# Expert stage: sums leave PSUM on ScalarE and are added into x on GpSimd, which also makes the token matrix; inner activations are turned two units later

## What is computed

```
aff = softmax(h @ w_router);  g, idx = top_k(aff.T, 2 * n_tok // 16)     # 64 latent, 16 prompt tokens
xe = xt[idx]
hid = silu(xe @ w1) * (xe @ w3)                                         # 1024 -> 1024, for each expert
ye = (hid @ w2) * g
out = zeros.at[idx].add(ye);  x = x + gate2 * out
```

## Time and profile before

| | us |
|---|---|
| median of three runs | 3389.22 (3378.01 to 3390.41) |
| profiled execution | 3387.95 |
| its span | 3386.2 |
| PE, PEld, DVE, ACT, POOL busy | 2982.3, 2085.9, 2172.3, 1564.4, 217.2 |
| one pair of experts, fourth of layer 0 | 79.1 |

### The profile page before, as it was taken

One profiled execution on the slowest core, in us unless ns is written; L12 is line 12 of the kernel. 1 busy time (PEld: TensorE's weight loads), 2 busy tenths in 40 slices (PEclk: granted clock), 3 DMA queues, 4 the chain that ended last, 5 costly groups with the idle time before them and its releaser, 6 DMA issues.

```text
span 3386.2 us, 42584 instructions
## 1 busy us (share of the span) xinstructions
PE 2982.3 (88%) x14726; PEld 2085.9 (62%) x14726; DVE 2172.3 (64%) x3151; ACT 1564.4 (46%) x2258; POOL 217.2 (6%) x272
## 2 busy tenths in 40 slices
PE   6979988988977999999878899889799599999995
PEld 3656755766645666666646576556575366666663
DVE  3364345566437999999834553455752699999994
ACT  3151333123125777777533413331410377777773
POOL 0050011011000000000002300110200000000000
PEclk9989999999988999999989899999999699999996
DMA  7203200321416999999811031023012299999991
GB/s 265 81 1 110 76 27 26 114 76 51 156 56 225 332 326 329 320 332 328 288 65 57 26 135 51 1 75 113 28 38 94 102 341 325 319 329 322 329 338 58
DMA packets 280112, 564.04 MB, mean 167 GB/s; under 512 B 14040, under 2 KB 19872, under 8 KB 279328
## 3 DMA queue, kind: packets, MB, share of 16 engines
q1 hardware_dynamic: 273056, 543.33, 45.4%
q10 hardware_dynamic: 4448, 9.87, 0.8%
q0 software_dynamic: 2464, 8.91, 0.7%
HBM read 546.44 MB, written 15.63 MB: 166 GB/s over the span
## 4 chain that ended last, share of the span: by engine, by line
PE 66%; DVE 16%; ACT 6%; issue 5%; DVEq 4%; ACTq 2%; DMA 1%; POOL 0%; POOLq 0%; SPq 0%
PE mm L1423 17%; PE mm L931 14%; PE mm L868 11%; DVE w_lo L1913 6%; PE mm L933 4%; PE mm L1166 2%; DVEq L2451 2%; PE mm L965 2%; ACT w_hi L1482 2%; DVE x L1921 2%; ACTq L1851 2%; PE oo L1188 1%; DVE scratch L2102 1%; PE tp L1175 1%; PE oo L905 1%
## 5 line engine op out<-in xcount | busy, mean ns | idle before, releaser
L1913 DVE TENSOR_TENSOR w_lo<-ring,w_hi 128x1024 fp32r<-128x1024 f32 x768 | 919.1, 1221 | 87.8 <-ACT w_hi L1482 57.7
L1482 ACT ACTIVATE w_hi<-ring 128x1024 fp32r<-128x1024 f32 x768 | 803.5, 1059 | 288.4 <-PE mm L1423 266.5
L1913 DVE TENSOR_TENSOR dw_lo<-ring,dw_hi 128x512 fp32r<-128x512 f32 (+1 forms) x168 | 114.9, 689 | 420.4 <-ACT dw_hi L1482 420.1
L1482 ACT ACTIVATE dw_hi<-ring 128x512 fp32r<-128x512 f32 (+1 forms) x168 | 104.4, 627 | 548.3 <-PE mm L933 543.5
L931 PE MATMUL mm<-h_hi,dw_lo 128*128 128x512 f32 (+1 forms) x672 | 328.9, 489 | 19.2 <-DVE dw_lo L1913 13.1
L933 PEld LDWEIGHTS mm<-h,ring 128*128 128x128 f32 (+1 forms) x1344 | 256.3, 191 | 61.3
L931 PE MATMUL mm<-h_hi,dw_hi 128*128 128x512 f32 (+1 forms) x672 | 269.4, 401 | 0.0
L931 PE MATMUL mm<-h_lo,dw_hi 128*128 128x512 f32 (+1 forms) x672 | 268.0, 399 | 0.0
L933 PE MATMUL mm<-h,ring 128*128 128x128 f32 (+1 forms) x1344 | 260.9, 276 | 0.0
L868 PE MATMUL mm<-scratch,ring 128*128 128x512 f32 (+3 forms) x896 | 257.9, 440 | 1.6 <-ACT scratch L1482 1.6
L1423 PE MATMUL mm<-w_lo,xa_hi 128*80 128x512 f32 x512 | 204.6, 400 | 15.5 <-DVE w_lo L1913 9.5
(11 more groups left out here) (256 smaller groups left out, 5011.9 us busy)
## 6 DMA issues: line engine op xcount, KB each, us to landing
ring<-in_w_ff SPq DMA_DIRECT2D x384, 1024.0 KB, 6.0
ring<-in_w_ada SPq DMA_DIRECT2D x48, 1024.0 KB, 7.3
ring<-in_w_gate SPq DMA_DIRECT2D x24, 1024.0 KB, 5.8
ring<-in_w_in SPq DMA_DIRECT2D x16, 1024.0 KB, 8.9
ring<-in_w_o SPq DMA_DIRECT2D x8, 1024.0 KB, 7.4
x_spill<-x SPq DMA_DIRECT2D x2, 2560.0 KB, 13.0
ring<-in_w_br_da SPq DMA_DIRECT2D x4, 1024.0 KB, 6.3
ring<-in_w_br_mla SPq DMA_DIRECT2D x4, 1024.0 KB, 6.2
```

The source lines that it names most:

```text
L1482: return act.activation(out, in_, ACT.Copy, scale=scale)
L1913: return dve.tensor_tensor(out, in0, in1, op)
```

## The change

1. `TURN_AT` goes from 10, 18, 26, 34 to 12, 20, 28, 36. `SLOTS_AT` moves with it from 20 to 22, `ROWS_AT` stays at 38.
2. `spread` leaves VectorE. ScalarE copies the sum out of PSUM with the gate as its scale, into one of two buffers (`tmp[2]` and `rstd`), and GpSimd adds the buffer into x. ScalarE's copy k stands ahead of w_hi of unit 12+k and waits until GpSimd has done addition k-2. GpSimd's additions of units 2n and 2n+1 stand behind its wait for chunk n. The last pair's sums are still added by VectorE, after a wait for GpSimd.
3. `hot_t` is made by GpSimd behind chunk 11, when all combines of the pair before are done. TensorE's first combine and VectorE's `slots` wait for it.
4. `hidden` on VectorE has no drain any more and signals `hid_ready` directly. `mm_empty` is raised by TensorE behind its wait for `hid_ready`.

```diff
-TURN_AT = [JOB_UNITS * (q + 1) + 2 for q in range(4)]
-SLOTS_AT, ROWS_AT = TURN_AT[1] + 2, TURN_AT[3] + 4
+TURN_AT = [JOB_UNITS * (q + 1) + 4 for q in range(4)]
+SLOTS_AT, ROWS_AT = TURN_AT[1] + 2, TURN_AT[3] + 2
+SPREADS = (PAIRS - 1) * KT
...
+        def spread_at(k):
+
+            return (tmp[2], rstd)[k % 2][:, 0:NLAT]
...
+            pool.sem_inc(spread_done, 2)
...
-                def pair(e, last_pair=False):
+                def spread(k, of):
+
+                    pool.wait_ge(spread_in, l * SPREADS + of * KT + (k + 1))
+                    pool.sem_inc(pool_waited, 1)
+                    pool.tensor_tensor(x[:, k, 0:NLAT], x[:, k, 0:NLAT], spread_at(k), ALU.add).then_inc(spread_done, 1)
+
+                def pair(e, before=None, last_pair=False):
                     for n in range(PAIR_CHUNKS):
 
                         pool.wait_ge(w_ready, pair_part(l, e, n * UNITS + UNITS - 1))
                         pool.sem_inc(chunks_free, 1)
+                        if before is not None:
+                            for m in (UNITS * n, UNITS * n + 1):
+                                if 0 <= m - SPLITS - COMBINE_AT < KT:
+                                    spread(m - SPLITS - COMBINE_AT, before)
+                        if n == after(TURN_AT[AF1]):
+                            if before is not None:
+                                wait_o_full(pool, l, OO["pairs"] + KT - 1, before)
+                            pool.sem_inc(pool_waited, 1)
+                            pool.tensor_scalar(hot_t[:, :], tokens, slot_tok, 1.0, ALU.is_equal, ALU.mult)\
+                                .then_inc(hot_t_ready, 1)
                         if n == after(SLOTS_AT) + 1 and not last_pair:
                             fetch(e + 1)
...
                     if k == 0:
                         pe.wait_ge(ye_done, l * PAIRS + of + 1)
+                        pe.wait_ge(hot_t_ready, l * PAIRS + of + 1)
...
                     pe.wait_ge(hid_ready, (l * PAIRS + e) * 4 + (q + 1))
+                    pe.sem_inc(mm_empty[job_turn(q) % 2], 1)
...
+                def spread(k, of):
+
+                    j = OO["pairs"] + k
+                    act.wait_ge(spread_done, l * SPREADS + of * KT + (k + 1))
+                    wait_o_full(act, l, j, of)
+                    copy(spread_at(k), oo[j % 2][:, :], mod[:, 40 + k, 0:1]).then_inc(o_empty[j % 2], 1)
+                    act.sem_inc(spread_in, 1)
+
+                def hi_of_chunk(n, e, before=None):
...
+                            if before is not None and 0 <= p - COMBINE_AT < KT:
+                                spread(p - COMBINE_AT, before)
...
-                        if before is not None and 0 <= m - SPLITS - COMBINE_AT < KT:
-                            spread(m - SPLITS - COMBINE_AT, before)
...
                     tt(hid[0:rows_, n * 512:(n + 1) * 512], mm[j % 2][0:rows_, 512:1024], tmp[n][0:rows_, 0:512],
-                       ALU.mult).then_inc(mm_empty[j % 2], 1)
-                    dve.drain()
-                    dve.sem_inc(hid_ready, 1)
+                       ALU.mult).then_inc(hid_ready, 1)
...
-                            ts(hot_t[:, :], tokens, slot_tok, ALU.is_equal)
                             lo_of_hidden(AF1, e)
                         if n == after(SLOTS_AT) and not last_pair:
+                            dve.wait_ge(hot_t_ready, l * PAIRS + e + 1)
                             slots(T_SLOTS, e, e + 1)
...
+                dve.wait_ge(spread_done, (l + 1) * SPREADS + 2)
                 for k in range(KT):
                     spread(k, PAIRS - 1)
```

More of the change, by code:

```diff
@@ L540, in build @@
         pool_waited = sem("pool_waited")
+        spread_in, spread_done = sem("spread_in"), sem("spread_done")
         xhi_ready, xe_ready = sem("xhi_ready"), sem("xe_ready")
@@ L544, in build @@
         ye_stored, ye_back, ye_done = sem("ye_stored"), sem("ye_back"), sem("ye_done")
-        ye_hi_ready = sem("ye_hi_ready")
+        ye_hi_ready, hot_t_ready = sem("ye_hi_ready"), sem("hot_t_ready")
         y_ready, y_sent = sem("y_ready"), sem("y_sent")
@@ L843, in _ @@
                 fetch(0)
-                with pool.Fori(0, PAIRS - 1) as e:
-                    pair(e)
-                pair(PAIRS - 1, True)
+                pair(0)
+                with pool.Fori(1, PAIRS - 1) as e:
+                    pair(e, e - 1)
+                pair(PAIRS - 1, PAIRS - 2, True)
         @block.tensor
@@ L1796, in _ @@
                 copy(hotw_pt.rearrange("p g s -> p (g s)"), tp[:, 0:2 * P]).then_inc(t_empty, 1)
-                def hi_of_chunk(n, e, last_pair=False):
+                def spread(k, of):
[5 more added lines that the diff above has]
+                def hi_of_chunk(n, e, before=None):
                     i = AT[l, "pairs"] + n
@@ L1855, in pair @@
                     for n in range(2, PAIR_CHUNKS if last_pair else PAIR_CHUNKS + 2):
-                        hi_of_chunk(n, e, last_pair)
+                        hi_of_chunk(n, e, before)
                         if n == 2 and before is not None:
@@ L2413, in outputs, with lo_of_chunk @@
                         dve.sem_inc(ye_done, 1)
-                def lo_of_chunk(n, e, before=None):
+                def lo_of_chunk(n, e):
                     i = AT[l, "pairs"] + n
@@ L2463, in pair @@
                     for n in range(2, PAIR_CHUNKS if last_pair else PAIR_CHUNKS + 2):
-                        lo_of_chunk(n, e, before)
+                        lo_of_chunk(n, e)
                         if n == 2 and before is not None:
```

## The result

The changed kernel takes 3449.14 us (median of 4 runs, 3446.87 to 3451.89), the one before 3389.1 beside it. The ratio is 1.0184, 95% interval 1.0164 to 1.0204: 1.8% slower, 60 us, where the forecast had 3437 us and a range up to 3475. The profiled run took 3446.87 us, its span 3445.1. Ratios in this document leave out one run of 11,389 us, among four of the version with the old turns, whose other three took 3494 to 3497.

What follows compares the result with a forecast made beforehand. TensorE was taken to set the pace, VectorE close behind. 14 pairs with sums at +3.9 us (+54.6) and two first pairs at -3 (-6) gave +49 on 3387.95, so 3437 us; range 3380 to 3475.

Steps and rivals of the forecast that it cites:

- The start of the loop: Expert stage, w_lo of unit 13 on VectorE: claimed to end near 1301.3 us, no longer behind an addition.
- The loop: Units 12 to 19: w_lo, GpSimd addition, ScalarE copy, w_hi in a chain, 5.8 us per two units against TensorE's 3.7.
- wake: GpSimd's delay between the end of w_lo and its addition, taken as 0.25 us per round.
- The port: Behind unit 19: additions 6 and 7 hold up four w_lo on VectorE by 2.48 us, delaying unit 22.
- Gives back 1.19: Later in the pair, TensorE's waits at turns BF0 and BF1 vanish: 0.70 and 0.49 us back.
- The turns' worth: Turning two units later covers TensorE's waits for AF1, BF0 and BF1: 2.46 us a pair saved.
- Its list of TensorE's stops: Unit 10 (0.88 us) and turns AF1 (1.27), BF0 (0.70), BF1 (0.49): together 3.3 us a pair.
- Rival 2: Units 12 to 22: GpSimd handovers bind, but additions don't hold up w_lo; net +1.8 us a pair, 3407 us; chance 0.24 with mixtures.
- Rival 1: Units 12 to 19: the GpSimd handovers are hidden, 3.3 us a pair go, 3336 us; chance 0.13.
- Rival 3: GpSimd is slow to wake, with register work at each wait: 3450 to 3496 us; chance 0.17.

Runs made afterwards that it cites:

- e8: Kernel before with turns two units later, no drain behind hidden, mm_empty raised by TensorE, VectorE's addition of sum 0 ahead of hidden AF0: 3355.23 us, ratio 0.9904.
- the last version: Kernel before with turns two units later, VectorE's additions one unit earlier, find_slots at unit 24, no drain, mm_empty by TensorE: 3335.28 us, ratio 0.9852.

## Why the prediction was right, point by point

**The verdict and the mechanism held.** 3437 was forecast, 3449 came. A pair is 83.8 us (forecast "about 83"), the first of a layer 3.1 shorter (forecast 3), the additions come in four groups of two, the copies 2, 4 and 6 wait for GpSimd, and TensorE stops at combines 4 and 6.

**The start of the loop** was right to 0.1 us: w_lo of unit 13 was to end 5.7 us behind the start of unit 8 (1301.3 against 1295.55), and it does.

**The loop was sized at 5.8 us and is 6.15.** By its terms: wake 0.35 (forecast 0.25), addition with handover 1.39 (1.34), copy to w_hi 0.59 (0.48), w_hi to copy 0.95 (0.97), copy to w_hi 0.57 (0.48), w_hi and w_lo 2.30 (2.28). The two copies are 0.2 of the 0.35 us missing: their length was taken from a copy of 128x512 without a scale, 0.60 us, and with the gate as scale it is 0.69. The rest is in the wake and the addition. The third loop took 6.36, since addition 4 took 1.49; two selections of 128x256 on VectorE run beside it, which is the likely reason. Three loops made 18.6 us and not 17.4, so unit 19 came 3.1 us later than before in this pair and 3.4 in the mean, where 1.8 was forecast.

**The port was put in the wrong place.** The forecast let additions 6 and 7 hold up the four w_lo by 2.48 us, and so unit 22. In the trace it is the other way round: VectorE ran its w_lo without a pause, and addition 6 took 5.93 us (row above). VectorE of that pair:

```profile
1325.84 0.68 DVE L1949 TENSOR_TENSOR scratch<-mm,tmp 80x512 f32<-80x512 f32 x1
1326.44 4.62 DVE L1949 TENSOR_TENSOR w_lo<-ring,w_hi 128x1024 fp32r<-128x1024 f32 x4
1330.98 0.48 DVE L1949 TENSOR_TENSOR hida_lo<-tp,hida_hi 128x320 fp32r<-128x320 f32 x1
1331.38 4.13 DVE L1949 TENSOR_TENSOR w_lo<-ring,w_hi 128x1024 fp32r<-128x1024 f32 x2
1337.52 0.16 DVE L2423 CAST stat<-tp 128x1 uint32<-128x1 f32 x1 [2.01 <-POOL hot_t L859]
```

Four w_lo in 4.62 us are undisturbed. Addition 6 ends 1.2 us behind the start of hida_lo, which has one input in PSUM, and so seems to have run only from there on. Unit 22 waits for find_slots, and that for hida_lo, none of which the additions had delayed. Unit 22 comes 6.7 us behind unit 19, 5.35 before: +1.35 in the mean, where the forecast had +3.3. And even this is not the port's: it is 6.6 us with fills in place of additions and 6.5 with the turns alone. It is the turn and find_slots with its wait, which have moved into this stretch. The two errors, in the mean 1.6 us too little in the loop and 1.95 too much behind it, nearly cancel: +4.8 measured, +5.1 forecast. The sum was right partly by that luck.

**"Gives back 1.19" did not come, and that is where the port costs.** From unit 22 on the pair is only 0.1 us shorter than before (39.9 for 40.0). It is 1.2 shorter in e8 (38.8), and with fills in place of additions too (38.8). So the late turns do give back what was forecast, and the additions take it away. In the trace above numbers 6 and 7 run late, the two w_lo beside them take 4.13 us and not 2.36, and hot_t, which stands behind them on GpSimd, ends late too. `slots` waits 2.0 us for it, with w_lo of the next units queued behind. TensorE pays for both at unit 26:

```profile
1337.84 0.39 PE L1448 MATMUL mm<-w_hi,xb_hi 128*128 128x512 f32 x1
1339.47 0.50 PE L1448 MATMUL mm<-w_lo,xb_hi 128*128 128x512 f32 x1 [1.25 <-DVE w_lo L1949]
```

That is 1.63 - 0.23 = 1.4 us. Four of the twelve middle pairs have this stop. Five have one of only 0.2 us there, but reach unit 22 1.1 us later. Three have no stop, but units 22 to 24 take 5.8 us and not 4.2. The kinds differ in where TensorE's granted clock falls: at units 14 and 15 (0.50 from 1317 to 1319), at 18 and 19 (0.63 from 1240.5 to 1243), or at 22 (0.50 from 2928 to 2930); no run shows what decides that. A pair is 83.7 to 83.9 us long in each kind. hot_t was costed at nothing ("hot_t on GpSimd holds w_lo for under a microsecond"). It takes 3.46 us in the mean, against 0.48 on VectorE, but by itself it doesn't stop TensorE: with the fills `slots` waits the same 2.0 us for a hot_t that is longer still, and TensorE does not stop at unit 26.

```profile
1327.24 4.18 POOL L861 TENSOR_SCALAR hot_t<-merged,stat 128x512 fp32r<-128x512 f32 x1 [2.90 <-DVE w_lo L1951]
```

It takes the late additions as well: there hot_t ends 3.1 us behind the start of unit 22, and in the changed kernel 4.85.

**The turns' worth.** 2.46 us were to go; alone they gave 0.9. They gave 3.7 in the last version, where find_slots has moved away from hida_lo and VectorE's queue is in order as well. The forecast had seen that find_slots still needs hida_lo, and priced nothing for it. Its list of TensorE's stops also left out two of 0.9 and 1.0 us, at units 6 and 44; they are in all twelve versions, so the forecast lost nothing by that.

**The rivals.** Rival 2, the loop without the port, gave +1.8 a pair by its working and +2.7 by the fills, and the change measured +4.7. It was right that additions 6 and 7 don't hold up the four w_lo in front of find_slots, and wrong that additions hold up none: those that nobody waits for cost 6.2 us a pair. Rival 1, the loop hidden, is answered by additions that start 6.1 us apart where TensorE needs 3.7, and by one column, which brings them to 5.06 apart and the pair down with it. Rival 3, the slow wake, needed 0.93 us and got 0.35.

The Trainium skill, page "SBUF — State Buffer", section "Who interferes with whom", says that a VectorE instruction of this kind and a GpSimd instruction that reads SBUF exclude each other, and that "Issue order, not op shape, decides who blocks". The exclusion is what the runs show (86 us for additions that nobody waits for). On who blocks the trace differs. Addition 6 starts at 1326.26 by the profile, beside the product (0.68 us at 1325.84), and the first w_lo at 1326.44, yet four w_lo passed it; the addition of one column was passed in the same way.

## What to carry to other kernels

Work moved to an idle engine has no cost in length, and two others: the handovers that it joins into a loop, and the port that it shares. Before moving it, write down who must be done before it may start and who waits for its end, and add up one round of that loop; it has to be under the time in which the leading engine does the same work, here 3.7 us. Shortening one step shows whether such a loop binds: here the round fell by just what the step lost. Read single instructions for that and not a group's mean: the mean of the one-column additions, 0.8 to 1.4 us, hides six that take about 0.2 and two that wait for the port. And where a stop is taken away by moving a step, look at the next step that needs the same buffer: 1.0 us of the 3.7 gained at last hung on find_slots, which had moved along at the same distance.

## What was not expected of the hardware

- VectorE kept GpSimd out over several instructions. An addition on GpSimd that takes 1.28 us alone took 5.93 beside four w_lo without a gap (1.14 us apart), and one of a single column 4.85. Where the two took turns, the addition took up to 2.3 us, and w_lo 1.5 to 2.3 and not 1.22.
- Additions of 128x1 took 0.19 us on GpSimd where VectorE left it alone, those of 128x512 1.28. A comparison of 128x512 (hot_t) took 2.1 to 4.3 us there in the mean of a run, and 0.48 on VectorE. It took 2.0 where it started behind two w_lo of VectorE (one column), and 4.2 where it started beside them, in the row above: they last 2.35, so it seems to have waited for both.
- A stop of TensorE of 1 us was followed by a stretch at a granted clock of 0.50 in some pairs of one program and not in others. It made the same pair 77.4 or 78.9 us long. In the changed kernel the clock falls to 0.66 in the 5 us that hold the stop of 1.9 us.
